# Experts, one block per turn: single rooms for tokens, hidden values and outputs, and a new order of the weight splits

## The reference

```python
h = jax.nn.silu(xb @ w_gate[e]) * (xb @ w_up[e])
return h @ w_down[e]
```

## Time and profile before

| what | value |
|---|---|
| time, median of 3 runs (lowest to highest) | 2530.02 us (2527.29 to 2530.62) |
| profiled execution, its own time | 2530.61 us |
| its span, first to last instruction | 2528.8 us |
| TensorE busy in the span | 2293.5 us, 91% |
| VectorE, ScalarE, GpSimd busy | 1409.1, 985.7 and 317.9 us |
| mean granted TensorE clock | 0.957 |
| expert stage, from the first gate product | 1635.29 us on |

### The profile page before, as it was taken

One profiled execution on the slowest core, in us unless ns is written; L12 is line 12 of the kernel. 1 busy time (PEld: TensorE's weight loads), 2 busy tenths in 40 slices (PEclk: granted clock), 3 DMA queues, 4 the chain that ended last, 5 costly groups with the idle time before them and its releaser, 6 DMA issues. The chain is left out here.

```text
span 2528.8 us, 34818 instructions
## 1 busy us (share of the span) xinstructions
PE 2293.5 (91%) x12079; PEld 1303.1 (52%) x12080; DVE 1409.1 (56%) x2049; ACT 985.7 (39%) x1424; POOL 317.9 (13%) x275
## 2 busy tenths in 40 slices
PE   4999999999959987999999998389999999999991
PEld 2465564655648973555555554244555455455540
DVE  5566565665548844333333332767557578667733
ACT  4522532333221333222222222246546577657733
POOL 0022121121230000000000000012121122112112
PEclk8999999999979999999999999599999999999996
DMA  5201001001050133111111101469668899898927
GB/s 191 88 12 65 9 26 59 1 26 44 9 208 26 51 141 118 50 44 58 67 67 42 51 34 42 171 231 323 216 226 296 288 321 321 314 319 298 321 75 280
DMA packets 151078, 349.50 MB, mean 138 GB/s; under 512 B 28608, under 2 KB 34112, under 8 KB 150720
## 3 DMA queue, kind: packets, MB, share of 16 engines
q1 hardware_dynamic: 136000, 310.32, 33.7%
q0 software_dynamic: 13824, 33.59, 5.8%
q10 hardware_dynamic: 1152, 4.19, 0.4%
HBM read 303.48 MB, written 61.34 MB: 144 GB/s over the span
## 5 line engine op out<-in xcount | busy, mean ns | idle before, releaser
L110 PE MATMUL bankA<-main_room,hnT 128*128 128x512 f16 (+1 forms) x1536 | 303.2, 356 | 5.5 <-DVE main_room L569 5.5
L110 PE MATMUL bankE<-wg,xT 128*128 128x512 f16 x1152 | 261.7, 384 | 19.9 <-DVE xT L2455 15.7
L110 PE MATMUL bankE<-wd,hT 128*128 128x512 f16 x1152 | 256.5, 379 | 1.7 <-DVE hT L2460 1.7
L110 PE MATMUL bankE<-wu,xT 128*128 128x512 f16 x1152 | 257.2, 380 | 0.0
L110 PEld LDWEIGHTS bankA<-main_room,hnT 128*128 128x128 f16 x1536 | 151.7, 99 | 148.7 <-issue 7.3
L110 PEld LDWEIGHTS bankE<-wg,xT 128*128 128x128 f16 x1152 | 113.8, 99 | 160.1 <-issue 28.0
L110 PEld LDWEIGHTS bankE<-wd,hT 128*128 128x128 f16 x1152 | 112.7, 98 | 137.6 <-issue 1.9
L110 PE MATMUL bankA<-hnT,main_room 128*128 128x512 f16 x768 | 172.2, 386 | 8.9 <-DVE hnT L545 8.9
L110 PEld LDWEIGHTS bankE<-wu,xT 128*128 128x128 f16 x1152 | 113.0, 98 | 125.9 <-issue 0.8
L110 PE MATMUL bankC<-w_probs,probsT 128*128 128x512 f16 x768 | 171.5, 380 | 0.0
L110 PE MATMUL bankC<-main_room,hnT_c 128*128 128x512 f16 x768 | 170.7, 379 | 0.0
(11 more groups left out here) (366 smaller groups left out, 3303.5 us busy)
## 6 DMA issues: line engine op xcount, KB each, us to landing
w_rows<-in_w_gate SPq DMA_DIRECT2D x64, 1024.0 KB
w_rows<-in_w_up SPq DMA_DIRECT2D x64, 1024.0 KB
w_rows<-in_w_down SPq DMA_DIRECT2D x64, 1024.0 KB, 11.2
x_room<-in_x SPq DMA_DIRECT2D x4, 2048.0 KB, 11.0
cat_t<-scratch_cat SPq DMA_DIRECT2D x16, 512.0 KB, 4.8
main_room<-in_x SPq DMA_DIRECT2D x16, 512.0 KB, 5.5
scratch_ybuf<-main_room SPq DMA_DIRECT2D x16, 512.0 KB, 2.6
out<-hf SPq DMA_DIRECT2D x16, 512.0 KB, 12.1
```

The costliest lines, as they stand in the source:

```text
L110: ins = pe.matmul(o, a[x][k], b[y][k], start=start and k == 0 and j == 0, stop=stop and k == n - 1 and j == 2)
```

## The change

One turn now does one block, and each of `xr`, `xT`, `sg`, `hT` and `y` exists once. The number of blocks done is turns + 2 with turns = blocks - 2, where before it was 2*turns + 2 with a rounded number of turns. `gather(b)` waits for `turn_x(b-1)`; TensorE transposes the next block's rows behind up instead of ahead of it. ScalarE and VectorE split the gate pieces ahead of the token splits, the up and down pieces behind them, all in one step. `first` on VectorE splits the tokens of block 1 ahead of the weights of slot 1. The last two adds stand outside the loop and take their rows from `rows_end`, for which VectorE does seven more small operations in `gates_listed`. The parts left out below only drop the index of the room.

```diff
-HB = 2
...
-MAX_TURNS = NB // HB - 1
-MIN_TURNS = (USED_MIN - 1) // HB
+MAX_TURNS = NB - 3
+MIN_TURNS = USED_MIN - 2
...
-LISTED = 18
+LISTED = 25
...
-        xr = [sb(f"xr{i}", [P, D]) for i in range(HB)]
-        xT = [sb(f"xT{i}", [P, 2, KT, P], F16) for i in range(HB)]
-        sg = [sb(f"sg{i}", [P, DE]) for i in range(HB)]
-        hT = [sb(f"hT{i}", [P, 2, FT, P], F16) for i in range(HB)]
-        y = [sb(f"y{i}", [P, D]) for i in range(HB)]
+        xr, xT = sb("xr", [P, D]), sb("xT", [P, 2, KT, P], F16)
+        sg, hT, y = sb("sg", [P, DE]), sb("hT", [P, 2, FT, P], F16), sb("y", [P, D])
...
-        rows_from, rows_to = sb("rows_from", [P, NB], U32), sb("rows_to", [P, NB], U32)
+        rows_from, rows_to, rows_end = sb("rows_from", [P, NB], U32), sb("rows_to", [P, NB], U32), sb("rows_end", [P, 2], U32)
+        at_end, end_f = work(0, NB), work(0, 2)
...
             def gather(b):
-                if b >= HB:
-                    pool.wait_ge(xt, 2 * (b - HB) + 2)
...
                 if b:
-                    pool.wait_ge(y_st[(b - 1) % HB], (b - 1) // HB * 16 + 16)
+                    pool.wait_ge(xt, 2 * b)
...
+            def add(b, rows):
+
+                if b:
+                    pool.wait_ge(y_st, b * 16)
                 pool.wait_ge(y_t, b * 2 + 2)
...
             gather(0)
             gather(1)
             pool.wait_ge(planned, 1)
             used = turns_used(pool)
-            for t in range(1, NT + LATE):
-                if t < USED_MIN // HB:
-                    gather(HB * t)
-                    gather(HB * t + 1)
-                elif t < NT:
-                    with pool.If(used + 1 > t):
-                        gather(HB * t)
...
-                elif t >= LATE:
-                    with pool.If(used + 1 > t - LATE):
-                        add(HB * (t - LATE))
-                        add(HB * (t - LATE) + 1)
-            for i in range(HB):
-                pool.wait_ge(y_st[i], used * 16 + 16)
+
+            def turn(b):
+                gather(b + 1)
+                if b >= 2:
+                    add(b - 2, rows_to[:, b - 2:b - 1])
+
+            for b in range(1, MAX_TURNS + 2):
+                if b < USED_MIN:
+                    turn(b)
+                else:
+                    with pool.If(used + 2 > b):
+                        turn(b)
+            pool.wait_ge(lists, LISTED)
+            for n, done in enumerate((y_st, end_st)):
+                pool.wait_ge(y_end, 2 * n + 2)
+                pool.indirect_dma_start(dram["ybuf"], bass.IndirectOffsetOnAxis(ap=rows_end[:, n:n + 1], axis=0), y[:, :], None,
+                                        bounds_check=T - 1, oob_is_err=False, compute_op=ALU.add).then_inc(done, 16)
+            pool.wait_ge(end_st, 16)
+            pool.wait_ge(x_ld, used * 16 + 48)
...
-                step(t * HB + 1, 1, t)
-                step(t * HB + 2, 0, t + 1)
-            last(used * HB + 1, used)
+                step(t + 1)
+            last(used + 1)
...
-            def gates_ups(b):
+            def gates(b):
 
                 def split(slot, v):
                     act.wait_ge(gd, b)
                     nearest(0, slot, v)
                     nearest(1, slot, v)
+                return split
+
+            def ups_downs(b):
+                def split(slot, v):
                     act.wait_ge(ud, b)
                     nearest(2, slot, v)
                     nearest(3, slot, v)
-                return split
-
-            def downs_(b):
-                def split(slot, v):
                     act.wait_ge(yd, b * 2)
                     nearest(4, slot, v)
                     nearest(5, slot, v)
                 return split
...
-            def take_y(b, i, k):
-                act.wait_ge(y_st[i], k * 16)
+            def take_y(b, taken=y_t):
+                act.wait_ge(y_st, b * 16)
...
                 for p in GU:
                     nearest(p, 1, 1)
-                take_x(1, 1)
-
-            def step(b, i, k):
-                following(act, b - 1, downs_(b - 1))
-                silu(b, i)
-                take_h(b - 1, 1 - i)
-                take_x(b + 1, 1 - i)
-                following(act, b, gates_ups(b))
-                take_y(b - 1, 1 - i, k if i else k - 1)
-
-            def last(b, k):
-                following(act, b - 1, downs_(b - 1))
-                silu(b, 1)
-                take_h(b - 1, 0)
-                take_y(b - 1, 0, k)
-                take_h(b, 1)
-                take_y(b, 1, k)
+                take_x(1)
+                for p in DN:
+                    nearest(p, 1, 1)
+
+            def step(b):
+                take_h(b - 1)
+                silu(b)
+                following(act, b, gates(b))
+                take_x(b + 1)
+                following(act, b, ups_downs(b))
+                take_y(b - 1)
+
+            def last(b):
+                take_h(b - 1)
+                silu(b)
+                take_y(b - 1, y_end)
+                take_h(b)
+                take_y(b, y_end)
...
-            for i in range(HB):
-                dve.memset(xr[i][:, :], 0.0).then_inc(x_clear, 1)
+            dve.memset(xr[:, :], 0.0).then_inc(x_clear, 1)
...
-            do(ts, turns_f[:, :], end[:, NE - 1:NE], 1.0 / HB, -0.5 - 0.25, ALU.mult, ALU.add)
-            do(ts, turns_f[:, :], turns_f[:, :], WHOLE, None, ALU.add)
-            do(ts, turns_f[:, :], turns_f[:, :], -WHOLE, float(MAX_TURNS), ALU.add, ALU.min)
+            do(ts, turns_f[:, :], end[:, NE - 1:NE], -2.0, float(MAX_TURNS), ALU.add, ALU.min)
...
             def gates_listed():
+                for n in range(2):
+                    note(dve.tensor_scalar, at_end[:, :], iota[:, 0:NB], 2.0 - n, end[:, NE - 1:NE], ALU.add, ALU.is_equal)
+                    note(dve.tensor_tensor, at_end[:, :], at_end[:, :], row_f[:, :], ALU.mult)
+                    note(dve.tensor_reduce, end_f[:, n:n + 1], at_end[:, :], AX.X, ALU.add)
+                note(dve.tensor_copy, rows_end[:, :], end_f[:, :])
...
-            def gate_up_rest(slot, v):
-                for p in GU:
+            def gate_rest(slot, v):
+                for p in GU[0:2]:
                     rest(p, slot, v)
 
             def down_rest(slot, v):
                 for p in DN:
                     rest(p, slot, v)
 
-            def product(b, i):
+            def up_down_rest(slot, v):
+                for p in GU[2:]:
+                    rest(p, slot, v)
+                down_rest(slot, v)
...
                 gates_listed()
                 down_rest(0, 0)
                 gates_taken()
-                product(0, 0)
-                gate_up_rest(1, 1)
-                x_rest(1, 1)
-
-            def step(b, i, k):
-                following(dve, b - 1, down_rest)
-                h_rest(b - 1, 1 - i)
-                x_rest(b + 1, 1 - i)
-                following(dve, b, gate_up_rest)
-                product(b, i)
-
-            def last(b, k):
-                following(dve, b - 1, down_rest)
-                h_rest(b - 1, 0)
-                product(b, 1)
-                h_rest(b, 1)
+                product(0)
+                x_rest(1)
+                gate_rest(1, 1)
+                up_down_rest(1, 1)
+
+            def step(b):
+                h_rest(b - 1)
+                following(dve, b, gate_rest)
+                product(b)
+                x_rest(b + 1)
+                following(dve, b, up_down_rest)
+
+            def last(b):
+                h_rest(b - 1)
+                product(b)
+                h_rest(b)
...
-                    pe.wait_ge(y_t, b * 2)
+                    if more:
+                        pe.wait_ge(y_t, b * 2)
...
-            def step(b, i, k):
-                def turns():
-                    turn_h(b - 1, 1 - i)
-                    turn_x(b + 1, 1 - i, k + 1 if i else k)
-
-                by_slot(b, gate_up(b, i, turns))
-                by_slot(b - 1, down(b - 1, 1 - i))
+            def step(b):
+                by_slot(b, gate_up(b, lambda: turn_h(b - 1)))
+                turn_x(b + 1)
+                by_slot(b - 1, down(b - 1))
 
             def first():
-                turn_x(0, 0, 0)
-                gate_up(0, 0)(0, 0)
+                turn_x(0)
+                gate_up(0)(0, 0)
                 gates_listed()
-                turn_x(1, 1, 0)
-
-            def last(b, k):
-                by_slot(b, gate_up(b, 1, lambda: turn_h(b - 1, 0)))
-                by_slot(b - 1, down(b - 1, 0))
-                turn_h(b, 1)
-                by_slot(b, down(b, 1))
+                turn_x(1)
+
+            def last(b):
+                by_slot(b, gate_up(b, lambda: turn_h(b - 1)))
+                by_slot(b - 1, down(b - 1))
+                turn_h(b)
+                pe.wait_ge(y_end, 2)
+                by_slot(b, down(b, False))
```

(81 more changed lines are left out.)

18 lines of the change are left out of this document (6 added, 12 removed).

## The result

The changed kernel takes 2511.35 us (median of 4 runs, 2509.53 to 2515.68) against 2529.76 before: ratio 0.9933, 95% interval 0.9918 to 0.9948. That is 18.4 us less where some 16 were forecast, and inside the range.

A forecast was written before the change was run, and what follows sets the result against it. TensorE was taken to set the time in the expert stage. Terms -16.85 -7.3 +0.3 +4.0 +3.2 = -16.65 us, from 2530.6, gave 2514 us; range 2507 to 2525.

The forecast's parts named there:

- Blocks: Expert stage: 47 blocks run instead of 48, one regular step less, -16.85 us.
- The 0.00 MB of the last add: End of the expert stage: the last add moved no data, so block 47, the 48th, holds no row.
- The other one: Gathers: the quickest landed after 3.1 us against a median of 8.2, taken as showing that block 47 is empty.
- Start: Start of the expert stage: token splits of block 1 come earlier on VectorE, gate(2) starts 7.3 us earlier.
- Regular step: Loop steps in the new order stay at 16.85 us, since gate(b+1) can start at 16.1 to 16.4.
- the cover: The 30 steps that split weights: 0.5 to 0.8 us to spare before the next gate.
- Late weights: Regular steps, one place: gate(30) 2.4 us late, 4.3 with lost clock, against 4.03 before; net +0.3 us.
- Exit: Leaving the loop: 16 unused turns walked instead of 8, at 0.5 us each, +4.0 us.
- Tail: End of the stage: the last add carries data, landing in 6.3 us against 3.1 when empty, +3.2 us.

The follow-up runs named there:

- memset run: The changed kernel with a memset of 128x1536 (about 1.4 us of VectorE) ahead of x_rest in every turn: 2537.49 us, ratio 1.0034 to the kernel before.
- the start alone: The kernel before with one edit, the token splits of block 1 ahead of the gate and up splits of slot 1: 2517.84 us, ratio 0.9964.
- own turns: The changed kernel with its loop running exactly the used turns (45) instead of 61 with 16 skipped: 2499.0 us, ratio 0.9886 to the kernel before.

## Why the prediction was right

**Blocks.** One regular step of 16.85 us less; the run with one block more gives it back. The 0.00 MB of the last add was the sign that held. The other one was misread: the gather that landed after 3.1 us is not that of block 47, for which the trace of before has no landing, but that of block 40, at 2283.65:

```profile
L2158 POOL DMA_INDIRECT xr<-scratch_xn_scr,rows_from x1: 1061/1061/1061, 2283.7 to 2283.7; - x1
...
DMA to landing us min/median/max: 3.1/3.1/3.1
```

**Start.** Gate(1) was forecast 8.33 us earlier and came 8.33 earlier (76.62 to 68.29). Down(0) waited 0.19 us, not 1.05, because gate(1), cold, took 6.86 us to its successor instead of 6.65, and the six splits were through somewhat sooner; so gate(2) gained 7.76 instead of 7.3.

**Regular step.** The forecast had ScalarE's first gate split 7.3 to 7.6 us behind the gate's start and the next gate ready at 16.1 to 16.4. In the step shown it is 7.55 and 15.84 + 0.35 = 16.2. The memset run shows that the cover was real and no larger. No gather was waited for in the loop, and the room y held ScalarE up to 8.1 us at times, where nothing hung on it.

**Late weights** is the term furthest off: +0.3 forecast, -3.0 measured. The step that failed is "the second gate piece landed only at 2150.05, 12.7 us behind its gate", which was carried over from the old order's trace. In the new order both gate pieces are in time there and the lateness falls on up and down pieces, which have more room: the gate forecast 2.4 us late came 0.39 late. That the gate pieces land earlier because the up pieces are now asked for later (6.1 us behind the gate pieces instead of 4.3, by SyncE's rows in both traces) fits, but no run tried it alone. Nor is all of the 3.0 the order's: the old order lost between 1.7 and 4.0, and by the means of all profiles the order is worth about 1.45.

**Exit** was mis-sized: +5.9 for +4.0. The cost of an empty turn was taken from ScalarE, 0.5 us; on TensorE it is 0.75. The Trainium skill ("Advanced Engine Details and Errata", Control Flow Timing), by whose branch times I had estimated 2.1 us for eight turns, is further off: the runs show 6.0. What a skipped turn holds besides its branches, no run tells.

**Tail.** +3.8 for +3.2: 3.1 for the add (11.13 us from its issue to `finish` where it was 8.01), 0.6 for the gate (7.33 from it to the transposes where it was 6.72), 0.1 for the rest. The size of the add's part was right by luck: its 3.1 us for an empty transfer was read from the gather of block 40. The empty last add has no landing in that trace; in the second profile of the kernel before it has one, of 2.7 us:

```profile
q0 software_dynamic: 144, 0.00, 1.0%
issues: line engine op xcount, KB each, median us to landing
scratch_ybuf<-y,rows_to POOLq DMA_INDIRECT x1, 2.7
```

The gate's 0.6 can't be put down to the longer wait, since the same gate took 7.74 in the second profile of the kernel before.

The terms' errors, +0.6, +1.9, -0.5 and -3.3, nearly cancel: 17.9 for 16.65. The sum was right in part by luck.

## What to carry to other kernels

Where an engine is busy without a hole, count its units of work first: the one empty block was worth more than all reordering in the loop, and was to be seen in a transfer of 0.00 MB. Where a queue in program order feeds the first product, put what that product waits for first; this was one swapped pair of lines, 8.2 us at the start. A loop of fixed length with skipped turns is paid for at its exit: ending the loop at the used number brought 2511.35 down to 2499.0 us, the fastest version here.

## What the runs showed of the hardware

A skipped turn of such a loop cost TensorE 0.75 us between 8 and 16 of them (gaps of 10.08, 9.31 and 4.10 us with 16, 15 and 8, and none with 0), and the idle time cost clock besides. The stretch behind the loop in the changed kernel, and the first 4.36 us of the gate that ended it (columns: busy time and instructions of PE, PEld, DVE, ACT and POOL, then granted clock, DMA share, GB/s):

```profile
2414.00:2424.00 10.00, 0.36 (x2) 0.00 (x0) 0.00 (x0) 0.60 (x1) 1.59 (x1) 0.73 0.35 52
2424.44:2428.80 4.36, 4.36 (x11) 1.60 (x12) 0.00 (x0) 0.00 (x0) 0.00 (x0) 0.50 0.00 0
```

TensorE stood idle for nearly all of the first row, whose granted clock is 0.73 in the mean, so part of it is at 1.2 GHz of 2.4. The gate starts at 0.50, that is 1.2 GHz, and took 7.33 us to its successor; with own turns, and no such idle time ahead, 5.18 at a granted clock of 1.00. How much such a gate loses did not follow the length of the wait here: behind 4.1 to 4.2 us idle it took 6.72, 6.86, 6.87 and 7.74, behind 9.31 it took 6.50, and behind 10.08 between 7.33 and 7.84.

An indirect transfer whose rows are all out of bounds still took 2.7 us to land (the last add of the kernel before, in its second profile and with the start alone), and one with 98 rows took 6.0.
